# Output projection, FFN's first and last weight passes: two token parts instead of one

## The reference

```python
x = x + rmsnorm(merged @ w_out, g_post_mix)                 # output projection, norm, residual
hf = rmsnorm(x, g_pre_ffn)
hf = jnp.square(jax.nn.relu(hf @ w_ff1)) @ w_ff2            # 1024 -> 4096 -> 1024
x = x + rmsnorm(hf, g_post_ffn)
```

## Time and profile before

| | us |
|---|---|
| median of 3 runs | 1369.13 (1367.11 to 1369.84) |
| span of the profiled execution | 1366.3 |
| TensorE matmuls busy | 1304.1 (95%) |
| VectorE busy | 747.2 (55%) |
| ScalarE busy | 410.9 (30%) |
| GpSimd busy | 56.5 (4%) |
| HBM read, written | 98.79 MB, 14.21 MB |

### The profile page before, as it was taken

The page is one execution under the profiler, slowest core; times in us unless marked ns, Lnnn a source line. Parts: engine busy times, 40 slices in busy tenths (PEclk is TensorE's granted clock), DMA queues, the critical chain, the costliest instruction groups (busy, mean ns, idle before and its releaser), DMA issues.

```text
span 1366.3 us, 22112 instructions
## 1 busy us (share of the span) xinstructions
PE 1304.1 (95%) x8736; PEld 1278.5 (94%) x8736; DVE 747.2 (55%) x1309; ACT 410.9 (30%) x584; POOL 56.5 (4%) x51
## 2 busy tenths in 40 slices
PE   3999999999999999999999999699999999999996
PEld 2999999989999999989999899699999999999996
DVE  3452359786967887879755542574234333323334
ACT  4432133223311331222136324333123113213342
POOL 1000000000000000200000000290000000000000
PEclk9999999999999999999999999789999999999998
DMA  7132152215222432223222242122222222222211
GB/s 205 61 117 73 56 167 71 86 63 152 71 78 80 135 86 78 62 78 92 78 78 62 71 142 81 31 63 77 78 66 73 83 71 77 77 77 62 75 35 77
DMA packets 192013, 114.28 MB, mean 84 GB/s; under 512 B 13743, under 2 KB 189063, under 8 KB 191922
## 3 DMA queue, kind: packets, MB, share of 16 engines
q1 hardware_dynamic: 170738, 93.00, 24.1%
q10 hardware_dynamic: 21184, 20.02, 4.6%
HBM read 98.79 MB, written 14.21 MB: 83 GB/s over the span
## 4 chain that ended last, share of the span: by engine, by line
PE 90%; DVE 3%; ACT 3%; issue 2%; DMA 1%; SPq 1%; ACTq 0%; DVEq 0%; POOL 0%
PE out L323 76%; PE bank L1345 10%; PE bank L1340 4%; DMA CV<-in_cache_conv 1%; DVE WK L866 1%; DVE XL L869 1%; DVE WL L278 1%; SPq L339 1%; ACT WK L500 1%; ACT CV L500 1%; PE out L1340 0%; ACT GH L500 0%; DVE WK L869 0%; ACT L500 0%; ACT WH L274 0%
## 5 line engine op out<-in xcount | busy, mean ns | idle before, releaser
L323 PE MATMUL out<-XH,WH 128*128 128x320 f32 (+1 forms) x1680 | 397.3, 318 | 14.9 <-DVE XL L869 9.3
L323 PE MATMUL out<-XH,WL 128*128 128x320 f32 (+1 forms) x1680 | 393.2, 315 | 0.0
L323 PE MATMUL out<-XL,WH 128*128 128x320 f32 (+1 forms) x1680 | 392.3, 315 | 0.0
L323 PEld LDWEIGHTS out<-XH,WH 128*128 128x128 f32 x1680 | 285.5, 191 | 19.0 <-issue 12.5
L323 PEld LDWEIGHTS out<-XH,WL 128*128 128x128 f32 x1680 | 286.7, 191 | 2.0 <-issue 1.3
L323 PEld LDWEIGHTS out<-XL,WH 128*128 128x128 f32 x1680 | 287.0, 190 | 0.9
L278 DVE TENSOR_TENSOR WL<-ST,WH 128x1024 fp32r<-128x1024 f32 x153 | 192.1, 1256 | 125.6 <-ACT WH L274 107.9
L869 DVE SCALAR_TENSOR_TENSOR CV<-WK,cwu,CV 128x512 f32 (+1 forms) x480 | 227.1, 542 | 0.4
L274 ACT ACTIVATE WH<-ST 128x1024 fp32r<-128x1024 f32 x153 | 161.3, 1054 | 186.9 <-PE out L323 183.2
L323 PE MATMUL out<-GH,WH 128*128 128x320 f32 x768 | 176.1, 310 | 6.0 <-DVE WL L278 4.6
L323 PE MATMUL out<-GL,WH 128*128 128x320 f32 x768 | 174.9, 309 | 0.0
(11 more groups left out here) (142 smaller groups left out, 589.1 us busy)
## 6 DMA issues: line engine op xcount, KB each, us to landing
ST<-in_w_in SPq DMA_DIRECT2D x65, 512.0 KB, 4.3
ST<-in_w_ff SPq DMA_DIRECT2D x64, 512.0 KB, 4.0
WK<-in_state_mlstm_C ACTq DMA_DIRECT2D x32, 256.0 KB, 2.8
o_C_sample<-WK ACTq DMA_DIRECT2D x32, 256.0 KB, 2.2
WK<-in_x_prompt SPq DMA_DIRECT2D x8, 512.0 KB, 5.8
ST<-in_w_branch_m SPq DMA_DIRECT2D x8, 512.0 KB, 4.7
ST<-in_w_branch_c SPq DMA_DIRECT2D x8, 512.0 KB, 4.0
ST<-in_w_out SPq DMA_DIRECT2D x8, 512.0 KB, 4.8
```

Source lines behind the costliest of these rows:

```text
L323: last = pe.matmul(out[s][:, h, 0:H], w[:, s, kk, :], x[:, kk, h * H:(h + 1) * H], start=(m < 2), stop=(m >= len(ms) - 2))
```

## The change

OUT, the first pass of the FFN's first half (`FF0`) and the last pass of its second half are done twice, for frames 0 to 383 (blocks 0, 1, 2) and for frames 384 to 639 (blocks 3, 4). A tile of a part has 24 matmuls (`gemm_part`). The weight tiles of these three stages are loaded and split twice, once for each part: 24 tiles more in the program. Each part has its own frame sums, power and spread. The first part's norm, residual and FFN input are worked out beside OUT's second part, and those of the second part beside FF0's first part; the instructions are laid into the order of ACT and DVE at fixed tiles. POOL now does all scalings and every other residual sum (L481's loop), and only then the squares and sums for the FFN's norm. `CV` is not zeroed any more: the first `w_ff2` pass, which is taken out of the loop, copies into it. In the last pass the first part's factors and its three output blocks are made by DVE in tiles 9 to 13, and blocks are stored in the order 0 to 4. The diff, cut to its core:

```diff
+PARTS = [(0, 3 * P), (3 * P, 2 * P)]
+BLOCKS = [(0, 1, 2), (3, 4)]
+    def gemm_part(pe, n, xh, xl, p, rhs_ready=None):
+        wait(pe, "w_lo", val(n) + 1)
+        wait(pe, f"of{n.par % 2}", ofcount(n))
+        for kk in range(KT):
+            if rhs_ready:
+                rhs_ready(kk)
+            for j, (w, x) in enumerate(((WH, xh), (WH, xl), (WL, xh))):
+                last = pe.matmul(gout_part(n, p), w[:, n.par % 2, kk, :], of_part(x[:, kk, :], p),
+                                 start=(kk == 0 and j == 0), stop=(kk == KT - 1 and j == 2))
+        last.then_inc(sem("tile_done"), 1)
...
 # SP
-            for r in range(4, KT):
-                load_tile(sp, N(N_OUT0 + r), w_o, 0, r * P)
+            for u in range(4, 2 * KT):
+                load_tile(sp, N(N_OUT0 + u), w_o, 0, u % KT * P)
+            for u in range(2 * KT):
+                load_tile(sp, N(N_FF0 + u), w_1, 0, u % KT * P)
...
 # POOL
+            for p in range(2):
+                g.wait_ge(sem("ovar"), p + 1)
+                g.tensor_tensor(sm[:, 6 + b0:6 + b1], sm[:, b0:b1], mhalf[:, b0:b1], ALU.pow).then_inc(sem("ort"), 1)
+                g.wait_ge(sem("orr"), p + 1)
+                for kk in range(KT):
...
+                    g.tensor_tensor(of_part(o_s[kk % 4], p), of_part(CV[:, kk, :], p), of_part(orr, p), ALU.mult
+                                    ).then_inc(sem("om"), 1)
+                    if kk % 2 == 0:
+                        g.wait_ge(sem("xa"), 2 * kk + 2)
+                        g.wait_ge(sem("om"), KT * p + kk + 1)
+                        g.tensor_tensor(of_part(MG[:, kk, :], p), of_part(o_s[kk % 4], p), of_part(MG[:, kk, :], p),
+                                        ALU.add).then_inc(sem("x2e"), 1)
+            g.wait_ge(sem("x2e"), KT)
+            g.wait_ge(sem("x2o"), KT)
             g.tensor_tensor(tmp[7], MG[:, 0, :], MG[:, 0, :], ALU.mult).then_inc(sem("fsum"), 1)
...
 # ACT
+            for u in range(2 * KT):
+                n, p, r = N(N_OUT0 + u), u // KT, u % KT
                 hi(n + 1)
+                if u > 11:
+                    ffn_input(0, 2 * (u - 12), 2 * (u - 11))
                 act.wait_ge(sem("tile_done"), val(n) + 1)
+                act.activation(of_part(tmp[u % 2], p), gout_part(n, p), ACT.Square).then_inc(sem("osq"), 1)
...
+                if u == 10:
+                    root_rows(0, B6[:, 0:3 * P])
+            for u in range(2 * KT):
+                n, p, r = N(N_FF0 + u), u // KT, u % KT
+                hi(n + 1)
+                if 3 < u < KT:
+                    ffn_input(1, 2 * (u - 4), 2 * (u - 3))
+                act.wait_ge(sem("tile_done"), val(n) + 1)
+                act.activation(of_part(tmp[4 + u % 2], p), gout_part(n, p), ACT.Relu).then_inc(sem(f"of{n.par % 2}"), 1)
+                act.wait_ge(sem("hsq"), u + 1)
+                copy(of_part(GH[:, r, :], p), of_part(tmp[2 + u % 2], p), "hh")
...
 # DVE
+            for u in range(2 * KT):
+                lo(N(N_OUT0 + u + 1))
+                if u > 11:
+                    residual(0, 2 * (u - 12) + 1)
+                    ffn_input(0, 2 * (u - 12))
+                    ffn_input(0, 2 * (u - 12) + 1)
+                add_up("osq", "oacc", tmp[6], u)
+                if u == 8:
+                    mean_squares(0, B4[:, 0:3])
+            for u in range(2 * KT):
+                n, p, r = N(N_FF0 + u), u // KT, u % KT
+                lo(n + 1)
+                if 3 < u < KT:
+                    residual(1, 2 * (u - 4) + 1)
+                    ffn_input(1, 2 * (u - 4))
+                    ffn_input(1, 2 * (u - 4) + 1)
+                evacuated(dve, n)
+                relu = of_part(tmp[4 + u % 2], p)
+                tt(of_part(tmp[2 + u % 2], p), relu, relu, ALU.mult).then_inc(sem("hsq"), 1)
...
+            def ffn_out():
+                for u in range(2 * KT):
+                    n, p, r = N(N_FF1 + 2 * KT * (DFF // D - 1) + KT + u), u // KT, u % KT
+                    if u < 2 * KT - 1:
+                        lo(n + 1)
+                    if u:
+                        add_up("ysq", "yacc", tmp[6], u - 1)
+                    dve.wait_ge(sem("tile_done"), val(n) + 1)
+                    tt(of_part(CV[:, r, :], p), gout_part(n, p), of_part(CV[:, r, :], p), ALU.add
+                       ).then_inc(sem(f"of{n.par % 2}"), 1)
+                    if u == 9:
+                        y_scales(0)
+                    if u == 10:
+                        y_roots(0)
+                        dve.wait_ge(sem("yt"), KT)
+                    if 10 < u < 14:
+                        y_out(u - 11)
...
 # TensorE
+            for u in range(2 * KT):
+                gemm_part(pe, N(N_OUT0 + u), XH2, XL2, u // KT,
+                          rhs_ready=(lambda kk: pe.wait_ge(sem("ml"), kk + 1)) if u == 0 else None)
+                if u == 1:
                     for c in range(1, 6):
                         pe.wait_ge(sem(f"xagain{c}"), 16)
...
+                if u == 8:
+                    pe.wait_ge(sem("xa"), 2 * KT)
+                    pe.wait_ge(sem("oacc"), KT)
+                    part_sums(tmp[6], B4, 0, "t_os")
+                if u == 10:
+                    part_spread(B6, 0, "t_or")
+            for u in range(2 * KT):
+                gemm_part(pe, N(N_FF0 + u), XH2, XL2, u // KT,
+                          rhs_ready=(lambda kk: pe.wait_ge(sem("fl"), u + kk + 1)) if u % KT == 0 else None)
```

More of the change, by code:

```diff
@@ L325, in gemm, with of_part, gout_part @@
         last.then_inc(sem("tile_done"), 1)
-    def o_scaled(kk):
-        return (tmp[4], tmp[5], tmp[1], tmp[3])[kk % 4]
+    o_s = [wk(off["so"] + i * T2, T2) for i in range(4)]
+    orr = wk(off["so"] + 4 * T2, T2)
+    def of_part(ap, p):
+        return ap[:, PARTS[p][0]:PARTS[p][0] + PARTS[p][1]]
+    def gout_part(n, p):
+        return out[n.par % 2][:, 0, 0:PARTS[p][1]]
+    def gemm_part(pe, n, xh, xl, p, rhs_ready=None):
[8 more added lines that the diff above has]
+        last.then_inc(sem("tile_done"), 1)
     OUTC = [TS + P * j for j in range(4)] + [0]
@@ L1274, in _, with add_up @@
[L1274 to L1290, removed]
+            def add_up(sq, name, acc, u):
+                p = u // KT
+                dve.wait_ge(sem(sq), u + 1)
+                if u % KT == 0:
+                    dve.tensor_copy(of_part(acc, p), of_part(tmp[0], p)).then_inc(sem(name), 1)
+                else:
+                    dve.wait_ge(sem(name), u)
+                    tt(of_part(acc, p), of_part(acc, p), of_part(tmp[u % 2], p), ALU.add).then_inc(sem(name), 1)
@@ L1305, in ffn @@
                     tt(tmp[2 + r % 2], tmp[4 + r % 2], tmp[4 + r % 2], ALU.mult).then_inc(sem("hsq"), 1)
-                    dve.wait_ge(sem("hh"), c * KT + (r + 1))
+                    dve.wait_ge(sem("hh"), c * KT + (KT + r + 1))
                     tt(GL[:, r, :], tmp[2 + r % 2], GH[:, r, :].bitcast(F32), ALU.subtract).then_inc(sem("hl"), 1)
-                for r in range(KT):
-                    if not last or r < KT - 1:
+                if not last:
+                    for r in range(KT):
@@ L1310, in ffn @@
                         lo(n + (KT + 1 + r))
[L1311 to L1318, removed]
+                        dve.wait_ge(sem("tile_done"), val(n + (KT + r)) + 1)
@@ L1319, in _ @@
+            with dve.Fori(1, DFF // D - 1) as c:
                 ffn(c)
@@ L1621, in ffn @@
             def ffn(c, last=False):
[L1622 removed]
+                n = N(N_FF1, 2 * KT, c)
                 if last:
                     pe.wait_ge(sem("fsum"), 2 * KT - 1)
[L1625 removed]
+                    frame_sums(tmp[7], B5, [P * i for i in range(5)], "t_fs")
                 for r in range(KT):
[L1627 removed]
+                    gemm(pe, n + r, XH2, XL2)
@@ L1628, in ffn @@
                     if last:
                         wait(pe, "x2t", 2 * r)
-                        by_frames(MG[:, r, :], B6, B7, "t_x2")
-                for r in range(KT):
-                    gemm(pe, n + (KT + r), GH, GL,
-                         rhs_ready=(lambda kk: pe.wait_ge(sem("hl"), c * KT + (kk + 1))) if r == 0 else None)
-                    if last and r:
-                        y_frames(r - 1)
-            def y_frames(r):
-                pe.wait_ge(sem("yg"), r + 1)
-                wait(pe, "yt", 2 * r)
-                by_frames(CV[:, r, :], B4, B5, "t_y")
@@ L1642, in _ @@
-            with pe.Fori(0, DFF // D - 1) as c:
+                        for i in range(5):
+                            tr(B6[:, P * i:P * i + P] if i < 4 else B7[:, 0:P], MG[:, r, P * i:P * i + P],
+                               "t_x2" if i == 4 else None)
+                if not last:
+                    for r in range(KT):
+                        gemm(pe, n + (KT + r), GH, GL,
+                             rhs_ready=(lambda kk: pe.wait_ge(sem("hl"), c * KT + (KT + kk + 1))) if r == 0 else None)
```

236 lines of the change are left out of this document (150 added, 86 removed).

## The result

The changed kernel takes 1379.32 us (median of 4 runs, 1376.73 to 1382.19), the kernel before 1368.95 in the runs beside it: ratio 1.0088, 95% interval 1.007 to 1.0107. It is slower, by 0.9%, with the whole interval above 1. The forecast was 1379.2 us, and slower.

A forecast was written before the change was run, and what follows sets the result against it. TensorE, busy 95% of the span, was taken as the bound. Stage +7.8, last pass +8.2 and tail -5.9 gave +10.1 us on 1366.3; with 2.8 us to the runs' median, 1379.2 us, range 1364 to 1388.

The forecast's parts named there:

- OUT, frames: Behind OUT's tile 1 TensorE waits 3.2 us for the last frame, landing 8.2 us after its issue.
- OUT, tiles 12 to 15: Split loop of 4.1 us a round, four rounds 16.4, plus 2.5 for POOL; first FFN tile starts at 880.3.
- FFN, tiles 0 to 7: First pass, 384 columns: 34.2 us, with loop and POOL costs 38.2, end 918.5.
- FFN, tiles 8 to 15: First pass, 256 columns: six tiles at 4.9 us beside POOL's sums, two at 3.4: 36.2 us, range 27 to 39.
- the dearer rival: Every low half and square waits for one POOL operation, 5.6 us a tile: 1382 to 1389 with fallen clock; chance 0.2.
- the rival of a full price and a fallen clock: Full POOL waits in every round, +13, and idle stretches dropping the clock to 1.2 GHz, +17 to +20; chance 0.2.
- Stage: OUT and the FFN's first pass, with the wait before the second pass: end 1011.5 against 1003.7, +7.8 us.
- Last pass: Loops of 4.6 us at 384 and 4.0 at 256: 68.8 us against 60.6 before, +8.2.
- Tail: After the last pass: fewer output rows -3.6, fewer block sums -1.2, narrower sum, square and adding -1.1: -5.9 us.
- Sum: Whole kernel: 7.8 + 8.2 - 5.9 = +10.1 us on a span of 1366.3; as median 1379.2.
- the free port: In the three disturbed stages POOL's operations mostly miss VectorE's, saving up to 13.5 us: 1365.7; chance 0.18.
- all splits are hidden: Weight splits stay hidden as in full-width stages, the bubble's 23 us is gained: about 1343 to 1346; chance 0.07.

The follow-up runs named there:

- frames_later: Changed kernel with the residual frames' transposes, and the copies behind them, one tile later; ratio 1.0049 to the kernel before.
- sums_later: Changed kernel with POOL's fifteen squares and sums for the FFN's norm started only after the narrow tiles; ratio 1.0000 to the kernel before.
- ahead: split_early with VectorE's low half of tile n+2 moved up too, and ScalarE evacuating first in the first pass; ratio .9996 to the kernel before.
- memsets: Changed kernel with POOL's sums of the FFN's norm replaced by 30 memsets, which read nothing; ratio 1.0010 to the kernel before.
- last_whole: Changed kernel with the last FFN pass whole again (eight tiles of 640, one tail); ratio 1.0058 to the kernel before.
- split_early: Changed kernel with ScalarE making tile n+2's high half when tile n is done, ahead of evacuating n, in all parted stages; ratio 1.0061 to the kernel before.
- all_parts: ahead plus POOL's sums after the narrow tiles and the frames one tile later; 1348.98 us, ratio .9884 to the kernel before.
- three_parts: Changed kernel with POOL's sums later, frames one tile later, and the early high half in the last pass alone; ratio .9928 to the kernel before.

## Why the prediction was right

**OUT, frames.** Forecast 3.2 us of waiting for the last frame, which lands 8.2 us after its issue; it was 2.79 and 8.3. frames_later shows that this time was on the path. It is not a fixed price. Other executions of the same order waited 1.41 to 2.77: in sums_later and ahead the last frame landed 7.0 us after its issue. In memsets and last_whole, behind waits of 2.7 us, the clock fell too: last_whole's ten transposes took 2.37 us instead of 1.28, at a granted clock of 0.57, which is most of the 1.26 by which its first stretch is longer than the changed kernel's.

**OUT, tiles 12 to 15.** Forecast start of the FFN 880.3; it was 882.00, less the 1.85 that came from ahead of OUT, 880.15. No run parts what these tiles paid to POOL from what their loop took, so the sum is borne out and its two terms are not; the same holds for the FFN's tiles 4 to 7.

**FFN, tiles 0 to 7.** Forecast 38.2 us; 882.00 to 919.66 is 37.7.

**FFN, tiles 8 to 15.** Forecast 36.2 us, measured 38.2 (919.66 to 957.87). I took 4.9 us a tile beside POOL, from a range of 4.9 to 5.6; it was 7.65 in the first, 5.3 to 5.6 in the next three, the dearer rival's price, and 4.25 in the fifth, under which POOL ended; the four low halves beside POOL paid 1.04 to 1.24 us each, nearly a full POOL operation. Five tiles stood under POOL and took 28.4 us; the other three took 9.8, 3.3 each, as forecast. TensorE's granted clock fell as well, behind the gap of 4.55 us; windows after, with length, busy us of PE, PEld, DVE, ACT, POOL, then clock and DMA:

```profile
926.00:932.00 6.00, 4.69 (x22) 4.69 (x23) 5.48 (x4) 1.36 (x2) 5.84 (x5) 0.50 0.33 90
```

The chain gives that tile 5.38 us and the one at 948.06, at full clock, 3.12:

```profile
927.31 5.38 PE out L349 x24
...
948.06 3.12 PE out L349 x24
```

This fall cost little by itself: had that tile ended earlier, the square behind it could have begun at 932.8, when the low half ahead of it on VectorE was done, and it began at 933.13. It fell again behind the gap of 2.25 us (0.70 in 938 to 941), and in OUT behind that of 3.12 (0.73 in 873 to 876); there VectorE, which the next tile waited for, did not wait for the slowed tile. So the falls came much as the rival of a full price and a fallen clock said, behind gaps of 2 to 5 us, and cost next to nothing, since VectorE and not TensorE set the pace. The mechanism, TensorE behind VectorE behind POOL's sums, is shown by sums_later and memsets.

**Stage.** +8.57 where +7.8 was forecast: the 2.0 us just named, less 0.15 in OUT, 0.5 in the first eight tiles, and the 0.5 us of wait ahead of the second pass, which was not paid (the chain runs through the 40 tiles from 957.87 on in 281.33 us).

**Last pass.** Forecast +8.2, measured +9.5: from 1293.34 + 7.05 + 0.54 = 1300.93 to VectorE's last sum at 1369.98, 69.05 us, the 68.8 forecast. The step that failed is the time of before. I took 8 x 7.58; its eight tiles have only six sets of transposes between them (the first two tiles follow each other without one, and the sets of the last two come behind), and ran from 1290.49 to 1350.06, 59.57: 8 x 7.035 + 6 x 0.55. The kernel after, chain:

```profile
1293.34 7.05 PE out L326 x48
```

and before:

```profile
1290.49 14.07 PE out L323 x96
```

That splits and not matmuls set the pace there, split_early shows: 4.06 to 3.09 us a tile.

**Tail.** Forecast -5.9, measured 1379.1 - 1369.98 = 9.12 against 16.2 from 1350.06 to 1366.3: -7.1. Timeline of DVE and PE after, against the earlier trace rows:

```profile
1369.98 0.42 DVE L938 TENSOR_TENSOR CV<-out,CV 128x256 f32<-128x256 f32 x1 [1.60 <-PE out L349]
1371.43 0.61 PE L1478 MATMUL bank<-onesd,WK 128*128 128x1 f32 x4 [1.27 <-DVE WK L938]
1373.45 2.48 DVE L941 SCALAR_TENSOR_TENSOR WK<-CV,sm,WK 128x1024 f32<-128x1024 f32 x2
```

The output rows gave the 3.6 us forecast. Sums and transposes gave more: before, they ran at half the clock,

```profile
1353.00:1356.00 3.00, 2.85 (x14) 2.45 (x13) 0.33 (x2) 0.21 (x2) 0.83 (x1) 0.50 0.00 0
```

and after, at a granted clock of 0.95 in 1370 to 1373. I took the 2.03 us of the earlier trace rows for the price of five blocks; last_whole did the same five in 1.28.

**Sum.** 8.57 + 9.48 - 7.12 = 10.9 against 10.1 forecast, and 1.85 from ahead of OUT. Two errors, of 1.3 us in the last pass and 1.2 in the tail, cancelled each other, and so did OUT and the narrow tiles in part; the hit to 0.1 us is luck, the sizes of the terms are not. Of the rivals, the full price was paid in four tiles, without the time that a fallen clock was to add; the free port is refuted (the port's price in tiles 8 to 15 alone is 10.4 us, more than the 9.0 I gave it); "all splits are hidden" was wrong for this kernel, but all_parts comes to 1349, near the 1343 to 1346 that it named, once the queues have the right order and POOL is out of the way.

## What to carry to other kernels

Cutting a tile in two doubles the work of those engines that prepare its weights, so before cutting, write down the loop that runs through them in queue order, and look at the place of the preparation on every engine of that loop: moved ahead on ScalarE alone it gained 7 us where VectorE's step stood first in its queue, and lost 4 where it stood behind other work. Look at what stands beside the cut tiles: work of POOL that wide tiles hid is what a narrow tile pays in full, and it can go beside other tiles. A forecast of a change between two stages needs a mark at each stage's end in both traces, since a term that hides a miscounted period or a slow clock only shows there.

## What the runs showed of the hardware

POOL beside VectorE's two-input operations: reading, it nearly doubles them (1.23 to 2.27 or 2.47) and is itself stretched (1.25 alone to 2.42); beside memsets of 0.69 us each, which only write, the low half keeps its 1.23.

After a short idle time the clock fell in some executions and not in others: the tail's ten sums took 2.03 us before (granted clock 0.50) and 1.28 in last_whole (1.00 in 1362.5 to 1363.8), each after 2.06 us of idling, and behind the frame's wait of 2.7 to 2.8 us it fell to 0.57 in last_whole and stayed at 1.00 in the changed kernel:

```profile
820.00:823.00 3.00, 2.34 (x17) 2.37 (x18) 0.00 (x0) 1.57 (x5) 0.00 (x0) 1.00 1.20 291
```

(the changed kernel's window; last_whole's:)

```profile
818.00:822.00 4.00, 3.27 (x15) 3.30 (x16) 0.00 (x0) 1.63 (x5) 0.00 (x0) 0.57 1.18 286
```

The same code ahead of OUT ended up to 4.4 us apart in ten executions (800.75 to 805.10). The window from 757 to 763 had a granted clock of 0.72 in the changed kernel and 1.00 before; but three_parts, at 0.72 as well, and split_early, at 1.00, are only 1.5 us apart. What else moves this start was not tried and stays open.
